# The FFNs of a two-block model as seven block products instead of eight, gate and up before down

## What is computed

```python
def swiglu(x, w_gu, w_down):
    gate, up = jnp.split(x @ w_gu, 2, axis=-1)
    return (jax.nn.silu(gate) * up) @ w_down

h = h + 0.5 * rmsnorm(swiglu(rmsnorm(h, norm_g[0]), ffn1_gu, ffn1_down), norm_g[1])
...   # mixer: h = h + rmsnorm(mixed @ w_out, norm_g[3])
h = h + 0.5 * rmsnorm(swiglu(rmsnorm(h, norm_g[4]), ffn2_gu, ffn2_down), norm_g[5])
gate = jax.nn.sigmoid(rmsnorm(h, norm_g[6]) @ ple_gate)
h = h + rmsnorm((p_i @ ple_proj) * gate, norm_g[7])
```

## Time and profile before

| | |
|---|---|
| time, median of 3 runs | 2553.77 us (2553.43 to 2554.87) |
| span of the profiled execution | 2551.0 us |
| the profiled execution's own time | not given apart; the median less the span is 2.8 us |
| PE busy | 2403.1 us (94%), 11424 records |
| DVE busy | 695.6 us (27%) |
| ACT busy | 341.5 us (13%) |
| DMA queue of the weights | 610 MB, 62% of 16 engines |

### The profile page before, as it was taken

One profiled execution on the slowest core, in us unless ns is written; L12 is line 12 of the kernel. 1 busy time (PEld: TensorE's weight loads), 2 busy tenths in 40 slices (PEclk: granted clock), 3 DMA queues, 4 the chain that ended last, 5 costly groups with the idle time before them and its releaser, 6 DMA issues.

```text
span 2551.0 us, 29433 instructions
## 1 busy us (share of the span) xinstructions
PE 2403.1 (94%) x11424; PEld 1455.9 (57%) x11424; DVE 695.6 (27%) x1578; ACT 341.5 (13%) x829; POOL 48.0 (2%) x95
## 2 busy tenths in 40 slices
PE   8999999999999999999999998889889998898987
PEld 6777647775677754777576543334437554344433
DVE  1112631112211263111232433223333343232333
ACT  1102230002100123000210200000003220000001
POOL 2000000000100000000000000000000000000000
PEclk9999999999999999999999999999999999999999
DMA  9443424433644342443374479999994278999998
GB/s 321 148 148 116 148 80 169 148 119 116 238 148 151 112 149 81 167 148 119 115 245 178 176 322 421 422 422 421 422 415 151 83 293 356 422 421 422 422 422 328
DMA packets 209278, 618.98 MB, mean 243 GB/s; under 512 B 15229, under 2 KB 120518, under 8 KB 161078
## 3 DMA queue, kind: packets, MB, share of 16 engines
q1 hardware_dynamic: 202144, 610.25, 62.0%
q0 software_dynamic: 1600, 5.06, 0.6%
q10 hardware_dynamic: 5462, 2.67, 0.4%
HBM read 616.89 MB, written 1.05 MB: 242 GB/s over the span
## 4 chain that ended last, share of the span: by engine, by line
PE 68%; DMA 23%; DVE 3%; SPq 2%; ACT 1%; issue 1%; DVEq 1%; POOL 0%; POOLq 0%; ACTq 0%
PE PS L2428 24%; DMA ring<-expert_parts 23%; PE PS L2438 12%; PE PS L1692 5%; PE PS L1596 4%; PE PS L1646 3%; PE PS L2480 2%; PE PS L2526 2%; PE PS L2677 2%; SPq L1052 1%; PE PS L1666 1%; PE PS L768 1%; PE PS L1201 1%; PE PS L2509 1%; PE PS L1718 1%
## 5 line engine op out<-in xcount | busy, mean ns | idle before, releaser
L2428 PE MATMUL PS<-xT,ring 128*128 128x256 f32 x2816 | 626.5, 381 | 5.3 <-DMA ring<-ffn_gate_up 2.8
L2428 PEld LDWEIGHTS PS<-xT,ring 128*128 128x128 f32 x2816 | 537.2, 191 | 113.9 <-issue 40.9
L1692 PE MATMUL PS<-ring,arena 128*32 128x512 f32 x1984 | 252.0, 655 | 68.1 <-DMA ring<-expert_parts 68.1
L2438 PE MATMUL PS<-ring,arena 128*128 128x512 f32 x704 | 315.9, 592 | 0.0
L1646 PE MATMUL PS<-arena,xn 128*128 128x128 f32 (+1 forms) x1536 | 271.4, 306 | 4.0 <-DVE arena L1404 4.0
L1646 PEld LDWEIGHTS PS<-arena,xn 128*128 128x128 f32 (+1 forms) x1536 | 215.4, 189 | 90.3 <-issue 31.7
L2137 DVE TENSOR_TENSOR arena<-PS,rb 128x256 f32<-128x256 f32 x88 | 37.4, 425 | 727.0 <-PE PS L2428 726.8
L2438 PEld LDWEIGHTS PS<-ring,arena 128*128 128x128 f32 x704 | 133.5, 190 | 132.6 <-issue 126.8
L1692 PEld LDWEIGHTS PS<-ring,arena 128*32 128x32 f32 x1984 | 66.8, 119 | 245.2 <-issue 153.5
L1505 DVE TENSOR_TENSOR h<-h,PS 128x1024 f32<-128x1024 f32 (+1 forms) x96 | 116.8, 1217 | 317.0 <-PE PS L1666 317.0
L1666 PE MATMUL PS<-arena 128*128 128x512 f32 (+1 forms) x384 | 188.7, 615 | 0.0
(11 more groups left out here) (394 smaller groups left out, 1755.5 us busy)
## 6 DMA issues: line engine op xcount, KB each, us to landing
ring<-expert_parts SPq DMA_DIRECT2D x368, 1024.0 KB, 14.8
ring<-ffn_gate_up SPq DMA_DIRECT2D x88, 1024.0 KB, 7.8
ring<-ffn_down SPq DMA_DIRECT2D x44, 1024.0 KB, 9.8
ring<-w_in SPq DMA_DIRECT2D x16, 768.0 KB, 5.5
ring<-conv_w_in SPq DMA_DIRECT2D x12, 1024.0 KB, 12.3
ring<-expert_parts SPq DMA_DIRECT2D x16, 512.0 KB, 10.2
ring<-w_out_rows SPq DMA_DIRECT2D x8, 768.0 KB, 7.0
ring<-ple_gate SPq DMA_DIRECT2D x8, 768.0 KB, 6.1
```

The costliest lines, as they stand in the source:

```text
L1692: last = mm(PS[BLK * j:BLK * (j + 1), 2, :], lhsT=xgT[:, k, j * BLK:(j + 1) * BLK], rhs=ahead_row(j, k) if is_ahead and half == 0 else gu[ ...
L2428: last = mm(PS[:, 4 + local % 4, s * 256:(s + 1) * 256], lhsT=w[:, s, k, j * P:(j + 1) * P], rhs=xT[:, k, META:T2], start=k == 0, stop=k = ...
L2438: return mm(PS[:, 2 * t + n, :], lhsT=hid[:, j, t * P:(t + 1) * P], rhs=w[:, j, n * 512:(n + 1) * 512], start=first, stop=final, skip_grou ...
```

## The change

The four FFNs are computed by Strassen's scheme (in the form with shared sums) on blocks of two by two: seven block products for eight.

- **Gate and up.** A unit is one 256-column gate part and one 256-column up part. The left matrix is the activations, split in tokens (tile 0, tile 1) and in features (0 to 511, 512 to 1023); the right one is split in features and in gate | up. `xT` tiles are now the stationary operand and the weights move, 256 columns at a time: seven products of four matmuls. Tokens come out on partitions, so SiLU takes the per-token factor as its scale and `spread` goes from the FFNs (it stays in the mixer).
- **Sums.** DVE builds the sums of activations once an FFN (four of 128x512) and the sums of weights in each unit (`weight_sums`, four of 128x1024; the first unit's are made earlier, in the mixer's end or in `ple`, except in the first FFN), and adds the products out of PSUM (`first_products`, `last_products`).
- **Hidden product.** It is turned by four PE transposes a unit (`hid_turn`), copied by ACT and kept in `hidT_` in SBUF for all 11 units.
- **Down** follows after all units: 11 steps `d` of seven matmuls of 512 columns, each product summed in a PSUM bank of its own over the steps; DVE makes four weight sums of 512 and four sums of 128 a step (`down_sums`). At the end DVE and ACT add the seven banks to the four pieces of the result (`ffn_post`).
- **Loads.** The parts of an FFN come in the order gate 0, up 0, gate 1, up 1, ..., then down 0 to 10. The very first part now counts on `final_loaded`, the second and third on `unit_loaded[0]`. The loops of the FFN on SP, PE, ACT and DVE are written out.
- **Start.** `turn=True`: the tile turns stand inside unit 0, the first product after the first four copies to `xT`.
- Semaphores of the second block are renamed and shared between its two layers, with other constants waited for.

```diff
     def load_first(parts):
-        for (dst, src), counted in zip(parts, (unit_loaded[0], unit_loaded[0], S.final_loaded)):
+        for (dst, src), counted in zip(parts, (S.final_loaded, unit_loaded[0], unit_loaded[0])):
...
 ACT
+        for u in range(FF_UNITS):
+            n = FF_UNITS * m + u
+            act.wait_ge(S.prod_done, 4 * n + 1)
...
+            a_.activation(p1, PS[:, X_BANK[u % 2], 0:256], ACT.Copy).then_inc(S.p1_copied, 1)
...
+            act.wait_ge(S.prod_taken, 4 * n + 1)
+            a_.activation(c11, c11, ACT.Silu, scale=rsh[:, 0:1]).then_inc(S.silu_ready, 1)
+            if u:
+                hid_copied(n - 1)
...
+            act.wait_ge(S.prod_taken, 4 * n + 4)
+            a_.activation(c21, c21, ACT.Silu, scale=rsh[:, 1:2]).then_inc(S.silu_ready, 1)
...
+        act.wait_ge(S.y_parts, 6 * m + 1)
+        a_.activation(tail_p1, PS[:, 4, :], ACT.Copy).then_inc(S.p1_copied, 1)
+        for i, u in enumerate((0, 1, 3, 2)):
+            act.wait_ge(S.y_made, 4 * m + i + 1)
+            y_square(u, tail_junk[:, u, :], xn[:, u // 2, 512 * (u % 2):512 * (u % 2) + 512])
 DVE
+    def weight_sums(l, u0, m, u):
...
+        if u >= 2:
+            dve.wait_ge(S.prod_done, 4 * (n - 2) + 4)
+        part_arrived(dve, l, u0, 2 * u)
+        part_arrived(dve, l, u0, 2 * u + 1)
+        v_.tensor_tensor(t1, b12, b11, ALU.subtract).then_inc(S.sums_ready, 1)
+        settle()
+        v_.tensor_tensor(t2, b22, t1, ALU.subtract).then_inc(S.sums_ready, 1)
+        settle()
+        v_.tensor_tensor(t4, b21, t2, ALU.subtract).then_inc(S.sums_ready, 1)
+        v_.tensor_tensor(b12, b22, b12, ALU.subtract).then_inc(S.sums_ready, 1)
...
+        if m == 0:
+            weight_sums(l, u0, m, 0)
+        weight_sums(l, u0, m, 1)
+        h_rstd(q, r)
+        first_products(0)
+        for u in range(1, FF_UNITS):
+            last_products(u - 1)
+            hidden(u - 1)
+            if u + 1 < FF_UNITS:
+                weight_sums(l, u0, m, u + 1)
+            else:
+                down_sums(l, u0, m, 0)
+            first_products(u)
+        last_products(FF_UNITS - 1)
+        down_sums(l, u0, m, 1)
+        hidden(FF_UNITS - 1)
+        for d in range(2, FF_UNITS):
+            down_sums(l, u0, m, d)
...
+    def ffn_post(l, i, n0, m):
...
+        v_.tensor_tensor(half(xn, 0), PS[:, 0, :], tail_p1, ALU.add).then_inc(S.y_made, 1)
+        dve.wait_ge(S.y_parts, 6 * m + 2)
+        v_.tensor_tensor(tail_u2, PS[:, 5, :], tail_p1, ALU.add).then_inc(S.tail_taken, 1)
+        settle()
+        dve.wait_ge(S.y_parts, 6 * m + 3)
+        v_.tensor_tensor(tail_u4, PS[:, 2, :], tail_u2, ALU.add)
+        settle()
+        dve.wait_ge(S.y_parts, 6 * m + 4)
+        v_.tensor_tensor(half(xn, 1), PS[:, 1, :], tail_u4, ALU.add).then_inc(S.y_made, 1)
+        gained(0)
+        dve.wait_ge(S.y_parts, 6 * m + 5)
+        v_.tensor_tensor(tail_u3, PS[:, 3, :], tail_u2, ALU.add)
+        settle()
+        gained(1)
+        mean_square(0)
+        v_.tensor_tensor(half(xn, 3), PS[:, 2, :], tail_u3, ALU.add).then_inc(S.y_made, 1)
+        dve.wait_ge(S.y_parts, 6 * m + 6)
+        v_.tensor_tensor(half(xn, 2), PS[:, 6, :], tail_u3, ALU.add).then_inc(S.y_made, 1)
+        updated(0)
+        gained(3)
+        gained(2)
+        mean_square(1)
+        updated(1)
...
         mixer(l)
+        dve.wait_ge(S.attn_done, 2 * l + 2)
+        weight_sums(l, U_FFN2, 2 * l + 1, 0)
         post(l, 1, 6, 1.0, lambda u: PS[:, u, :])
 PE
+    def product(out, a, b, slot=None):
+        for k in range(4):
+            last = mm(out, lhsT=a[:, k, :], rhs=b[:, 256 * k:256 * (k + 1)], start=k == 0, stop=k == 3)
...
+    def unit(u):
...
+        if u >= 2:
+            pe.wait_ge(S.prod_taken, 4 * (n - 2) + 4)
+        if u == 0:
+            if turn:
+                tile_turn(q, 0)
+            pe.wait_ge(S.xT_act, 3 * q + 1)
+        part_arrived(pe, l, u0, 2 * u)
+        product(PS[:, x, 0:256], a11, b11, done if u else None)
+        if u == 0:
+            if turn:
+                tile_turn(q, 1)
+            pe.wait_ge(S.xT_act, 3 * q + 2)
+        product(PS[:, x, 256:512], a12, b21).then_inc(S.prod_done, 1)
...
+        pe.wait_ge(S.sums_ready, 4 * n + 3)
+        product(PS[:, z_, 256:512], a22, t4)
...
+        product(PS[:, y, 0:256], s1, t1)
+        if u:
+            hid_turn(n - 1)
+            pe.wait_ge(S.prod_taken, 4 * (n - 1) + 2)
...
+        product(PS[:, W_BANK, 0:256], s2, t2).then_inc(S.prod_done, 1)
+        pe.wait_ge(S.sums_ready, 4 * n + 4)
...
+        product(PS[:, y, 256:512], s3, t3).then_inc(S.prod_done, 1)
...
+        product(PS[:, z_, 0:256], s4, b22).then_inc(S.prod_done, 1)
...
+        for d in range(1, FF_UNITS - 2):
+            pe.wait_ge(S.down_ready, FF_UNITS * m + d + 1)
+            last = down(d, 1)
...
+            if d == 1:
+                hid_turn(n)
```

More of the change, by code:

```diff
@@ L399, in build @@
         sgm = take(0, [2, D])
-        pleT = take(2048, [2, 256])
+        pleT = take(7552, [2, 256])
         def xcol(t):
@@ L482, in several @@
             return [[ctx.enter_context(nc.semaphore(f"moe{i}_{name}{j}")) for j in range(n)] for i in range(DEPTH)]
-        slot_free = several("slot_free", SLOTS)
+        slot_free = [ctx.enter_context(nc.semaphore(f"slot_free{j}")) for j in range(SLOTS)]
         gu_loaded, gu_used = several("gu_loaded", 2), several("gu_used", 2)
@@ L1445, in moe_vec @@
             settle()
[L1446 removed]
+            v_.tensor_tensor(sums[:, 4, :], sums[:, 3, :], msel[:, 2, :], ALU.add).then_inc(S.vec_step, 1)
             v_.tensor_tensor(tab, e12, first_slot.unsqueeze(1).unsqueeze(1).to_broadcast([P, 2, 3, NE]), ALU.mult)
@@ new lines, in down_sums @@
+            def down_sums(l, u0, m, d):
+                w = part_of(u0, 2 * FF_UNITS + d)
+                b11, b12, b21, b22 = [w[:, 512 * i:512 * (i + 1)] for i in range(4)]
+                t1, t2, t4, s1, s2, s4 = down_sums_of(d)
+                a11, a21, a12, a22 = [hidT_[:, d, f, t, :] for f in range(2) for t in range(2)]
+                if d < 2:
+                    dve.wait_ge(S.prod_done, 4 * (FF_UNITS * m + FF_UNITS - 2 + d) + 4)
+                else:
+                    dve.wait_ge(S.down_done, (FF_UNITS - 2) * m + d - 1)
+                dve.wait_ge(S.hidT_ready, FF_UNITS * m + d + 1)
+                part_arrived(dve, l, u0, 2 * FF_UNITS + d)
+                v_.tensor_tensor(t1, b12, b11, ALU.subtract)
+                v_.tensor_tensor(s1, a21, a22, ALU.add)
+                settle()
+                v_.tensor_tensor(t2, b22, t1, ALU.subtract)
+                v_.tensor_tensor(s2, s1, a11, ALU.subtract)
+                settle()
+                v_.tensor_tensor(t4, b21, t2, ALU.subtract)
+                v_.tensor_tensor(s4, a12, s2, ALU.subtract)
+                v_.tensor_tensor(b12, b22, b12, ALU.subtract)
+                v_.tensor_tensor(a21, a11, a21, ALU.subtract).then_inc(S.down_ready, 1)
@@ L2337, in ple @@
                 dve.wait_ge(S.proj_done, l + 1)
+                if l + 1 < DEPTH:
+                    weight_sums(l + 1, U_FFN1, 2 * l + 2, 0)
                 def half(u):
```

442 lines of the change are left out of this document (264 added, 178 removed).

## The result

| | before | after |
|---|---|---|
| time, median of 4 runs of each | 2554.32 us (2553.43 to 2559.37) | 2462.82 us (2462.07 to 2472.31) |
| span of the profiled execution | 2551.0 us | 2460.8 us |
| ratio, 95% interval | | 0.9648 (0.963 to 0.9666) |
| PE busy | 2403.1 us | 2309.6 us |
| DVE busy | 695.6 us | 1130.7 us |

The kernel became 91.5 us faster by the medians, 90.2 by the two profiled spans. Three of the four executions of the kernel after lie between 2462.07 and 2463.06 us, with a mean granted clock of TensorE of 0.979 to 0.98; the fourth took 2472.31 with 0.975. A clock lower by 0.004 over 2461 us is some 10 us, as much as that difference (an estimate from these means); no trace of that execution was kept, so its place is not known. In what follows a difference of a few microseconds between medians has to be read with this in mind.

A forecast was written before the change was run, and what follows sets the result against it. PE's column count was taken to bound the FFNs. PE work -96.1, first start +4.2, other starts -5.1, tails +6.2 and clock +1.0 gave -89.8 us: span 2461.2, time 2464 us, range 2452 to 2490.

The forecast's parts named there:

- Columns, -113.7: Gate/up and down matmuls of the four FFNs: 264 fewer 256-column pieces at 0.431 us each, -113.7 us.
- Transposes, +19.4: Each of 44 gate/up units: four added PE transposes turn the hidden product, 0.44 us a unit, +19.4 us.
- spread, -1.8: Four FFNs: the per-token scale becomes an ACT/DVE operand, so four PE records go from each, -1.8 us.
- What must hide under PE: Gate/up unit: DVE's 8.6 us, some 9.5 with drains, fits under PE's 12.5; down step: 4.1 under 6.0; no cost.
- first rival: Gate/up units: DVE sets the pace if a 1024-wide sum exceeds 2.0 us; 2574 us at 2.6; chance 4%.
- signs at the end of the prediction: Expected profile: 12.5 us per gate/up unit, no PE idle before products except unit 0 of the first FFN.
- PE loses between products: Gate/up units: straight code and eight waits instead of two cost 0.5 us a unit, 22 us: 2486; chance 8%.
- Starts: FFN starts: first +4.2 us, waiting for weight sums and loads; other three -5.1 together (-1.6, -1.9, -1.6).
- Tails: Four FFN ends: adding the down products delays what follows, +2.0 after each FFN1, +1.1 after each FFN2; +6.2 us.
- Clock, +1.0: Four FFN tails: gaps of 3 to 3.6 us between matmuls lower PE's granted clock, +1.0 us, bounds 0 and 8.
- second rival: The clock falls at every tail and start: +10 us, 2474 us, to 2480 if low for longer; chance 14%.

The follow-up runs named there:

- run 1: Kernel after with an eighth product again in each gate/up unit and down step, its result unused: 2575.09 us, ratio to before 1.008.
- run 2: Kernel after with the four transposes of the hidden product issued twice in each unit: 2482.41 us, ratio to before 0.9723.
- run 4: Kernel after with four extra 128x1024 weight sums on DVE in each gate/up unit: 2522.53 us, ratio to before 0.9876.
- control: The kernel after once more, without any edit, beside the last two runs on the same chip: 2463.84 us, ratio to before 0.9646.
- run 5: Kernel after with a semaphore of its own for the first up part, so the first weight sums needn't wait for the third load: 2464.61 us.
- run 8: Kernel after with the first up part counted alone and unread matmuls at the start (7), third FFN's start, FFN1 tails and mixers: 2460.38 us.
- run 7: Kernel after with unread matmuls in PE's waits: 15 at the first start, 4 ahead of the third FFN, 4 in first and third tails: 2465.87 us.
- run 9: Kernel after with the unread matmuls of run 7 plus four ahead of the wait in each mixer: 2462.32 us, ratio to before 0.9627.

## Why the prediction was right

**Columns, -113.7.** Held: 2464 + 616 records, 0.430 us for 256 columns, and 112.3 us when they are given back (run 1).

**Transposes, +19.4, spread, -1.8.** The first was measured at +19.6 by run 2 (0.43 us for four). The second wasn't tried alone; the second and fourth FFN stages meet the sum of their steps within 0.1 us, which leaves room only for errors that cancel.

**What must hide under PE.** Held, with 4.0 us to spare a unit. DVE's unit is 8.5 us by run 4, where the prediction's first rival counts 9.5 with drains. The four weight sums take 4.9 of them in the trace of after (49.68 to 54.59), so the rest is 3.6 us for the prediction's 4.6, and the point at which a 1024-wide sum decides is (12.53 - 3.6) / 4 = 2.2 us, not 2.0. The duration was 1.225, the one of the earlier trace rows. PE is idle ahead of a product in unit 0 alone, 7.0 us in the first FFN, but also 3.4 us in all in the other three, for copies to `xT`, which the signs at the end of the prediction leave out.

**PE loses between products.** Refuted: the period is 12.53, no gap. The code of a unit has seven waits, not eight.

**Starts.** The first: +5.3 by the profile (35.28 is 1.1 later than forecast), for +4.2. The control's third product started at 22.92 for 24.60, so this term moves with the landing of the loads by 1.7 us from one execution to the next, and +4.2 lies inside. Its cause is in the main the shared count, 3.8 us of the third product by runs 5 and 8. Two others: -25.5 for a forecast of -25.6 with the -1.6 in it. The third's slow start was forecast as well: its first product at 3.57 us.

**Tails.** The two behind FFN2 +1.04 and +1.03, +1.1 forecast. The third FFN's fits the forecast within 0.3. The first FFN's stage is 2.2 us longer than the steps say, 1.1 from the start and 1.1 from the clock (3.04 - 1.97).

**Clock, +1.0.** Mis-sized in its place rather than its sum: it is +1.1 in the first tail, nothing in the others, and -1.6 in mixer 2, where the kernel before had it low and the kernel after not. The sum, -0.5, is 1.5 us off. The prediction reads the earlier trace rows as a fall behind transposes alone; by its own window PE was busy for only 2.89 of the 6.50 us before, with waits of 2.49 and 0.83 us in them. So the row doesn't tell the transposes from the idle time, and neither does any run here. It also sets the 32 records' lengths in the timeline (8.81 and 7.14) against 6.91 of the chain; a steady group is 7.07 in the timeline, which makes the losses 1.7 and 0.1 us instead of 1.9 and 0.2. All terms together missed the span by 0.4 us (2460.8 against 2461.2), which is luck beyond some 2 us: the first start alone moves by 1.7. The forecast of 2464 us takes 2.8 us around the span; the profiled execution has 1.8 (2462.59 - 2460.8), and this 1.0 us is most of the 1.2 by which the median came lower.

**The second rival** was priced at 2474 us. The median doesn't show it, but the fourth execution of the kernel after, 2472.31 us at a clock of 0.975, has that size. In which stage it lost them isn't known.

## What to carry to other kernels

Before trading matmuls for additions, write down two sums for the repeated unit: what PE then needs, and what the engine that adds needs; while the second was smaller, here, a column that went was worth its full pitch, and order, loop form and operand origin cost nothing. The additions are paid where there is no PE work to stand beside: at the first unit and at the tail, here about 1 to 5 us each. The scheme costs 22 us before it gains 112. Most of this, the 19.6 for the transposes, goes with the number of units as the gain does; only the starts and tails, some 5 us, stay when the FFN is smaller (an estimate; no run has another size). Before believing a difference of 2 or 3 us between medians, look at the stage's length in a trace, and at the granted clock and the landing of the loads in both executions.

## What was unexpected of the hardware

The same wait of 2.05 us ahead of the same matmuls costs nothing in one execution and 1.6 to 1.7 us in another (before, runs 1 and 7), 5.3 us in run 4, through the granted clock (1.2 instead of 2.4 GHz); a wait of 1.98 us cost 4.6 us in run 9's second block, where after's of 1.96 cost nothing. What decides it stays open: no run here varies one wait's length with all else kept. Executions of one and the same kernel differ too. The five of run 9 took 2457.36 and 2457.74 us with a mean granted clock of 0.982 and 0.983, and 2462.32 to 2463.39 us with 0.979 and 0.98. So it is not shown either that filling one wait moves the fall to a later one: in run 7 the tails were whole and both mixers slow, in runs 8 and 9 the mixers were whole and the second block longer, but each of these is one execution, and run 1 had a longer mixer and a longer second block without any filler. The gain of runs 8 and 9 in the first block, 4.2 to 4.9 us, is therefore not safe in the total; the best version measured, run 8, stands at 2460.38 us beside 2463.84 of the kernel after on the same chip, with intervals that overlap.
